# Router logits in four column tiles, exp and the counts out of the ranking's way, and four weight items split in advance

## What is computed

```python
logits = (xt @ w_router + b_router).astype(F32)      # xt (264, 1024), w_router (1024, 8)
top_val, top_idx = lax.top_k(logits, TOP_K)          # TOP_K = 2 of 8 experts
gate = jax.nn.softmax(top_val, axis=-1)
...
counts = jnp.bincount(expert, length=N_EXPERTS)
padded = (counts + MOE_ROWS - 1) // MOE_ROWS * MOE_ROWS      # MOE_ROWS = 128
...
y_rows = lax.map(expert_block, (x_rows, blk_expert))  # swiglu(xb, w_gate[e], w_up[e], w_down[e])
```

## Time and profile before

| | us |
|---|---|
| median of 3 runs | 1290.85 (1290.51 to 1290.99) |
| the profiled execution | 1297.05 |
| its span | 1295.4 |
| busy: PE, DVE, ACT, POOL | 1250.1, 1038.1, 923.4, 78.1 |
| from the end of the attention (466.00) to item 2 of block 0 (521.50) | 55.5 |
| first expert block, from 521.50 | 82.5 |

### The profile page before, as it was taken

One profiled execution on the slowest core, in us unless ns is written; L12 is line 12 of the kernel. 1 busy time (PEld: TensorE's weight loads), 2 busy tenths in 40 slices (PEclk: granted clock), 3 DMA queues, 4 the chain that ended last, 5 costly groups with the idle time before them and its releaser, 6 DMA issues.

```text
span 1295.4 us, 21488 instructions
## 1 busy us (share of the span) xinstructions
PE 1250.1 (96%) x7324; PEld 1068.8 (83%) x7324; DVE 1038.1 (80%) x1463; ACT 923.4 (71%) x1330; POOL 78.1 (6%) x77
## 2 busy tenths in 40 slices
PE   6999999999997989999999999999999999999997
PEld 6989999999975767788888888888888888887885
DVE  6667766567539855998998998997998998998995
ACT  5755454456475774987987987887888888887783
POOL 1000000004301001100000000000000000002600
PEclk9989999999997988999999999999999999999998
DMA  8555445556569545998998998998998998998940
GB/s 350 196 211 193 167 179 196 195 195 241 167 225 381 225 163 200 410 421 338 414 400 325 403 403 319 416 401 323 413 397 328 415 391 330 417 387 323 409 184 34
DMA packets 59999, 391.50 MB, mean 302 GB/s; under 512 B 6718, under 2 KB 12994, under 8 KB 21474
## 3 DMA queue, kind: packets, MB, share of 16 engines
q1 hardware_dynamic: 51298, 354.29, 69.5%
q0 software_dynamic: 8640, 36.40, 7.6%
HBM read 367.41 MB, written 27.45 MB: 305 GB/s over the span
## 4 chain that ended last, share of the span: by engine, by line
PE 81%; DVE 10%; ACT 4%; issue 3%; DMA 1%; DVEq 0%; ACTq 0%; SPq 0%
PE bank L1931 17%; PE bank L1933 17%; PE bank L1932 17%; PE bank L1529 8%; PE bank L1530 8%; PE bank L1531 8%; DVE w_lo L1399 2%; PE bank L1916 1%; DVE d_lo L988 1%; ACT arena L735 1%; DMA ring<-in_wd 1%; ACT w_hi L851 1%; PE bank L1741 1%; PE bank L1865 1%; DVE arena L1226 1%
## 5 line engine op out<-in xcount | busy, mean ns | idle before, releaser
L1399 DVE TENSOR_TENSOR w_lo<-raw,w_hi 128x1024 fp32r<-128x1024 f32 x528 | 623.4, 1223 | 32.9 <-ACT w_hi L851 14.8
L851 ACT CAST w_hi<-raw 128x1024 fp32r<-128x1024 f32 x528 | 543.3, 1056 | 86.8 <-PE bank L1933 85.7
L1931 PE MATMUL bank<-w_hi,xg_hi 128*128 128x512 f32 x704 | 274.9, 391 | 1.6 <-DVE w_lo L1399 1.6
L1933 PE MATMUL bank<-w_hi,xg_lo 128*128 128x512 f32 x704 | 274.4, 390 | 0.0
L1932 PE MATMUL bank<-w_lo,xg_hi 128*128 128x512 f32 x704 | 273.9, 389 | 0.0
L988 DVE TENSOR_TENSOR d_lo<-ring,d_hi 128x1024 fp32r<-128x1024 f32 x120 | 148.1, 1240 | 84.8 <-ACT d_hi L606 81.0
L1529 PE MATMUL bank<-hA_hi,d_hi 128*128 128x264 f32 x640 | 184.6, 288 | 12.4 <-DVE hA_lo L978 8.9
L1530 PE MATMUL bank<-hA_lo,d_hi 128*128 128x264 f32 x640 | 182.1, 285 | 0.0
L1531 PE MATMUL bank<-hA_hi,d_lo 128*128 128x264 f32 x640 | 182.0, 284 | 0.0
L606 ACT CAST d_hi<-ring 128x1024 fp32r<-128x1024 f32 x120 | 125.0, 1045 | 76.2 <-PE bank L1531 68.4
L1931 PEld LDWEIGHTS bank<-w_hi,xg_hi 128*128 128x128 f32 x704 | 132.1, 188 | 29.4 <-DVE w_lo L1399 2.2
(11 more groups left out here) (334 smaller groups left out, 1509.3 us busy)
## 6 DMA issues: line engine op xcount, KB each, us to landing
raw<-in_moe SPq DMA_DIRECT2D x264, 1024.0 KB, 6.6
ring<-in_wd SPq DMA_DIRECT2D x29, 2048.0 KB, 8.4
out_rows<-zeros POOLq DMA_DIRECT2D x1, 6656.0 KB, 39.6
slot_rows<-zeros POOLq DMA_DIRECT2D x1, 6144.0 KB, 26.8
out_rows<-yrow POOLq DMA_DIRECT2D x8, 512.0 KB, 7.1
xs<-slot_rows POOLq DMA_DIRECT2D x7, 512.0 KB, 3.7
arena<-in_cmp_pages POOLq DMA_DIRECT2D x16, 128.0 KB, 3.4
X2v<-in_cmp_pages POOLq DMA_DIRECT2D x16, 128.0 KB, 2.8
```

Of the source, the lines that this page charges most:

```text
L851: nc.scalar.copy(w_hi[:, i % NSPLIT, :], raw[:, u % NRAW, ITEM * (i % 2):ITEM * (i % 2) + ITEM])\
L1399: V.tensor_tensor(w_lo[:, i % NSPLIT, :], raw[:, (i // 2) % NRAW, ITEM * (i % 2):ITEM * (i % 2) + ITEM], w_hi[:, i % NSPLIT, :].bitcast(F3 ...
L1931: T.matmul(out, lhs_hi, hi, start=first, stop=False)
L1933: return T.matmul(out, lhs_lo, hi, start=False, stop=last)
```

## The change

The router's weights are put into a buffer 32 columns wide, of which 8 are used and the rest is zero. Chunk k goes to column tile k % 4, so that the logits lie as four partial sums on partitions 0 to 7, 32 to 39, 64 to 71 and 96 to 103; steps 0 to 3 are issued together behind product 5, steps 4 to 7 behind product 7. Matmuls with a constant that has a one where partition mod 32 is the expert turn them to token rows and sum the four. The ranks are signalled apart from the counts, which go to another bank. The exp is issued behind the first items, and the gates that need it are computed in the last block. `AHEAD` is 4; the count of blocks is read after block 0's rows are rounded.

```diff
-AHEAD = 2
+AHEAD = 4
...
+    put("four", p % 32 == np.arange(NE)[None, :])
...
-        lgT = sb("lgT", [NE, NT])
+        lgT = sb("lgT", [P, NT])
...
             nc.gpsimd.memset(zeros[:], 0.0).then_inc(zeros_ready, 1)
+            nc.gpsimd.memset(wide_router[:], 0.0)
...
             pool.dma_start(kv_out, kvT).then_inc(kv_stored, 16)
+            pool.wait_ge(params_in, 32)
+            nc.gpsimd.tensor_copy(wide_router[:, :, 0:NE], w_router).then_inc(ws_ready, 1)
...
             act.wait_ge(lT_done, 1)
-            nc.scalar.copy(lgT[:, :], MISC[0:NE, 0:NT]).then_inc(lT_ready, 1)
+            nc.scalar.copy(lgT[:, :], MISC[:, 0:NT]).then_inc(lT_ready, 1)
...
-            act.wait_ge(rank_in, 1)
-            nc.scalar.activation(sc[:, :, 4:5], sc[:, :, 3:4], ACT.Exp).then_inc(exp_ready, 1)
...
             for i in range(AHEAD):
                 round_item(0, i)
-            act.wait_ge(blk_ready, 1)
-            last = act.value_load(blkinfo[0:1, MAXB + 1:MAXB + 2], min_val=1, max_val=MAXB - 1)
+            act.wait_ge(rank_in, 1)
+            nc.scalar.activation(sc[:, :, 4:5], sc[:, :, 3:4], ACT.Exp).then_inc(exp_ready, 1)
...
                 n = AHEAD
-                for _ in range(2):
-                    round_item(t, n)
-                    n += 1
                 rows_out(t)
...
             gathered(0, 0, (STAT, T0))
             gathered(0, 1, (STAT, T0))
+            act.wait_ge(blk_ready, 1)
+            last = act.value_load(blkinfo[0:1, MAXB + 1:MAXB + 2], min_val=1, max_val=MAXB - 1)
...
-            dve.wait_ge(exp_ready, 1)
-            settle(V.tensor_scalar(sc[:, :, 5:6], sc[:, :, 4:5], 1.0, None, ALU.add))
-            settle(V.reciprocal(sc[:, :, 6:7], sc[:, :, 5:6]))
-            V.tensor_tensor(sc[:, :, 7:8], sc[:, :, 4:5], sc[:, :, 6:7], ALU.mult)
...
-            counts = MISC[:, 48:56]
+            dve.wait_ge(rank_done, 2)
+            counts = B[0][:, 48:56]
...
             def early_and_last():
+                dve.wait_ge(exp_ready, 1)
+                settle(V.tensor_scalar(sc[:, :, 5:6], sc[:, :, 4:5], 1.0, None, ALU.add))
+                settle(V.reciprocal(sc[:, :, 6:7], sc[:, :, 5:6]))
+                settle(V.tensor_tensor(sc[:, :, 7:8], sc[:, :, 4:5], sc[:, :, 6:7], ALU.mult))
...
-            for i in range(AHEAD):
+            rest_item(0, 0)
+            gathered(0, 0, (STAT, T0))
+            rest_item(0, 1)
+            gathered(0, 1, (STAT, T0))
+            for i in range(2, AHEAD):
                 rest_item(0, i)
             dve.wait_ge(blk_ready, 1)
             last = dve.value_load(blkinfo[0:1, MAXB + 1:MAXB + 2], min_val=1, max_val=MAXB - 1)
-            gathered(0, 0, (STAT, T0))
-            gathered(0, 1, (STAT, T0))
...
-                for _ in range(2):
-                    rest_item(t, n)
-                    n += 1
...
-                i = T.matmul(MISC[0:NE, 0:NT], w_router[:, k, :], hB[:, k, :], start=(k == 0), stop=(k == KC - 1))
+                rows_ = slice(32 * (k % 4), 32 * (k % 4) + 32)
+                i = T.matmul(MISC[rows_, 0:NT], wide_router[:, k, :], hB[:, k, :], start=(k < 4), stop=(k >= 4))
...
-                if c >= 2:
-                    logits(c - 2)
-            logits(KC - 2)
-            logits(KC - 1)
+                if c == 5:
+                    pe.wait_ge(ws_ready, 3)
+                    for k in range(4):
+                        logits(k)
+            for k in range(4, KC):
+                logits(k)
...
-                i = T.transpose(MISC[0:z_ - a_, 8 * u:8 * u + 8], lgT[:, a_:z_], ident[0:NE, 0:NE])
+                i = T.matmul(MISC[0:z_ - a_, 8 * u:8 * u + 8], lgT[:, a_:z_], const("four"), start=True, stop=True)
...
-                T.matmul(out, before[0:r, 0:r], both[t], start=(t == 0), stop=True)
+                i = T.matmul(out, before[0:r, 0:r], both[t], start=(t == 0), stop=True)
+            i.then_inc(rank_done, 1)
+            pe.wait_ge(ht_ready, 1)
             for t, (a, z) in enumerate(spans):
-                i = T.matmul(MISC[:, 48:56], ones[0:z - a, 0:P], both[t], start=(t == 0), stop=(t == 2))
+                i = T.matmul(B[0][:, 48:56], ones[0:z - a, 0:P], both[t], start=(t == 0), stop=(t == 2))
             i.then_inc(rank_done, 1)
```

More of the change, by code:

```diff
@@ L83 @@
                       ("cmpmask", 30), ("sdist", PAST + NS), ("scdist", NS * NCMP), ("negslope", 1),
-                      ("iota", P), ("down8", NE), ("blk", MAXB * NE)])
+                      ("iota", P), ("down8", NE), ("blk", MAXB * NE), ("four", NE)])
 VECTORS, NVEC = layout([("mean", P), ("eps", 2), ("mix0", 8), ("mix1", 8), ("ffn0", 8), ("lng", 8), ("lnb", 8), ("kvn", 8), ("w00", 8)])
@@ L156, in build @@
         tok_rstd = sb("tok_rstd", [P, 4])
+        wide_router = sb("wide_router", [P, KC, 32])
         warm = sb("warm", [1, 2])
```

## The result

| | before | after |
|---|---|---|
| median, us | 1290.85 (5 runs) | 1284.35 (5 runs, 1283.43 to 1287.83) |
| profiled execution / its span, us | 1297.05 / 1295.4 | 1283.69 / 1282.1 |

What follows compares the result with a forecast made beforehand. PE was taken to set the pace in the output projection and blocks, with gains only where it stands still, mainly routing. Terms -2.9 - 3.3 + 0.6 = -5.6 us took 1290.85 to 1285.2 us, range 1283.0 to 1288.0.

Steps and rivals of the forecast that it cites:

- Part 1: Output projection: logits steps grouped by four in column tiles, eight records in 0.6 us; gain 2.9 us.
- Rival 2: Output projection: column tiles of full 128-row contraction overlap badly, gain there only 1.3 us, total 1287.3 us; chance 0.08.
- Part 2: Routing: removing the waits for counts and exp together lets the gather begin earlier; gain 1.15 us.
- Rival 4: Routing: PE's counts or DVE's block info remain the gate and item 4 waits; 1288.5 us, chance 0.06.
- Part 3: Routing into block 0: four items prepared in advance remove PE's wait before item 2; 3.3 us together with Part 2.
- case B: Gather: clock rises earlier, DVE's xg_lo half 0 sets PE's start, item 4 at 520.1; Part 2 and Part 3 gain 4.3.
- the cases: Gather: low clock covers as much as before (gain 2.0 to 3.0 us), or case B (4.3); 3.3 taken.
- rival 3: Gather: clock falls earlier against the work, staying low throughout; Part 2 and Part 3 give 0.1, total 1288.4 us; chance 0.07.
- Part 4: Last block: the gates' three steps in DVE's queue lengthen PE's wait for item 12; cost 0.6 us.
- rival 5: Seven block ends: two casts and rests delay item 4 or yrow, decisive from 0.8 us a block; 1294.4 us, chance 0.05.
- my own sign of being wrong: Expert blocks: the forecast counts as wrong if the period of the blocks moves; it expected the periods as before.
- rival 1: Whole kernel: outcome as forecast, 1285.2 us, its own range 1286.5 to 1284.2; chance 0.74.

Runs made afterwards that it cites:

- kernel 1: On the kernel before, only the router logits in column tiles; 1289.16 us (11 runs), ratio 0.9968.
- kernel 2: On the kernel before, only the exp moved behind the first items and the gates into the last block; 1292.06 us (one run).
- 3: On the kernel before, only the ranks signalled apart from the counts, which go to another bank; 1293.29 us (one run).
- kernel 4: On the kernel before, both routing edits together: exp and gates moved, ranks signalled apart from counts; 1292.33 us, ratio 0.999.
- 9: On the changed kernel, items 62, 63 and 64 of every block issued ahead of the last silu and hm; 1282.96 us (6 runs), ratio 0.9923.
- 11: 9 with the last block's early_and_last and last_weights one step later, gates staying in the last block; 1283.33 us (6 runs), ratio 0.9929.
- Kernel 8: kernel 7 with the last block's remaining small work one loop step later; 1286.64 us (8 runs), ratio 0.9951.
- kernel 10: Kernel 8 and 9 together: gates ahead of the loop, small work later, three items early at block ends; 1282.84 us (6 runs), ratio 0.9920.
- kernel 5: On the kernel before, only the four items in advance with their order in routing and blocks; 1288.17 us (one run).
- kernel 6: The changed kernel with two items in advance as before instead of four; 1288.01 us (12 runs), ratio 0.9959.
- kernel 7: The changed kernel with the gates on DVE ahead of the loop over the blocks instead of in the last block; 1287.82 us (one run).
- kernel 12: kernel 10 with DVE reading the count of blocks ahead of the last two splits instead of behind the gates; 1282.40 us (6 runs), ratio 0.9922.

## Why the prediction was right, and where a size was off

**Part 1, right in every term.** 2.9 us forecast, 2.92 measured, in after and alone in kernel 1. The group was taken at 0.6 us and has 0.59; the price behind it was taken at 0.20 and is 0.20. Steps 4 to 7 and the summing matmuls cost nothing: add 7 to the ranks is 6.81 us in both. Rival 2 (tiles overlap badly) falls. The Trainium skill (TensorEngine Tiling (Array Packing), Restrictions and Gotchas) lists the fast weight load as excluded by column tiling; by the reading of that line that I weighed against row L1674, the group would have taken 0.9 us, and it took 0.59. The summing matmuls are 0.4 us longer on PE than the transposes (0.74 against 0.31), not 0.3, and hidden as forecast.

**Part 2, right.** 1.15 us forecast, 1.24 measured. That both waits must go together was the step to test, and kernels 2, 3 and 4 show it (3.64, 3.48, 2.31). Rival 4 falls with it: block info is done 6.34 us behind the ranks' start, forecast 512.5 - 505.89 = 6.6.

**Part 3, right in its mechanism, mis-sized.** "I take 3.3 for both parts" is the term that was off: parts 2 and 3 gave 1.24 + 1.66 + 1.77 = 4.67 us. It is case B: the clock did not fall in the gather at all, and DVE's xg_lo half 0 releases item 0 (a wait of 0.37 us, named so in the row). The forecast of case B was 4.3; item 4 came 13.86 us behind the ranks where it had 520.1 - 505.89 = 14.2. Most of the difference is the counts: I had DVE begin them 0.25 us late behind PE, but with PE at full clock they were there. The choice between the cases was put at a value between them, where none of the profiles with parts 2 and 3 and the gates left in the last block lies (after, 9 and 11 gained 4.7 us). Kernel 8 against 10 prices the pair: 2.6 us; I had 4.3 - 2.0 = 2.3. The 0.10 us a record at the high clock was read too low: 26 records took the 2.85 us of rows 9, 0.11 each, and after has the same; case B does not hang on it.

**The reason for the clock was the wrong one.** I took a value "towards B since the idle time next to the gather goes", and let the 1.54 us ahead of the ranks stand in rival 3 as the thing "which stays". The kernels show the reverse. In every profile with a low stretch the clock falls amid the ranks or counts, before PE's wait for Gw has begun. Kernel 1 has part 1 and not part 2; its table has the fall at the counts, 2.7 us ahead of the gather:

```profile
500.45:501.20 0.75, 0.74 (x6) 0.74 (x6) 0.00 (x0) 0.73 (x2) 0.00 (x0) 1.00 0.00 0
501.20:504.17 2.97, 1.88 (x13) 1.69 (x13) 1.53 (x10) 2.96 (x4) 0.00 (x0) 0.54 0.00 0
```

So the wait that part 2 removes comes too late to be its cause. And the idle time ahead of the ranks did not stay: in after it is 1.08 us. The six summing matmuls of part 1 take PE longer than the three transposes did, and the ranks wait for DVE all the same. In after:

```profile
492.02 0.74 PE L1845 MATMUL bank<-consts_sb,lgT 128*128 128x8 f32 x6
```

and in kernel 2, with the old transposes:

```profile
497.13 0.31 PE L1840 MATMUL bank<-consts_sb,lgT 8*128 8x8 f32 x3
...
501.31 0.39 PE L1855 MATMUL bank<-lg,consts_sb 128*128 128x8 f32 x2 [1.53 <-DVE sc L1325]
```

Sorted by that idle time: all five profiles with 1.53 or 1.54 us (before, 2 to 5) had the clock low in the routing; of the nine with 1.08 or 1.09 (after, 1, 6 to 12) only kernels 1 and 10 had. The work that I had priced at 0.3 us and found hidden thus goes with 2.6 us of gain. It goes with it and doesn't guarantee it, kernel 10 being the code of kernel 8 up to there. That it is the cause is not shown: it was not tested by changing that idle time alone, and the profiles can be sorted another way too. Kernel 1 has the shorter idle time without part 2, kernel 4 has part 2 without the shorter idle time, and both are low; of the eight profiles with both, seven are high. So having both fits better than the idle time by itself (all six profiles that lack one are low), although PE does the same up to the fall in kernel 1 as in after. Rival 3 (low clock for the whole gather) came true nowhere: in kernel 10 the gather took 8.14 us, with the low clock over its first 5.3 us.

The clock also explains why the parts alone don't add up: kernel 4 gave 0.64 us from the ranks to item 4 and kernel 5 1.57, 2.2 together against 4.67. The missing 2.5 are about its price; kernel 6, with parts 1 and 2 and a high clock, gained 3.5.

**Part 4, right.** +0.6 forecast, 1.55 - 0.96 = +0.59 measured, and 1.58 and 1.59 in kernels 4 and 2, which have the gates there and not the rest. That it is the gates and no other work is shown by kernels 7 and 1, 3, 5 (0.93 to 0.97). The block ends cost nothing by the four items (kernel 5: 94.35), so rival 5 falls.

**Not foreseen.** The block's period is 94.42 us instead of 94.35, 0.5 us over seven blocks. Every kernel with the new logits and the old block ends has it (94.40 to 94.43), kernel 1 among them; none without them has it (94.33 to 94.35). What it does there is open: the part changes no instruction of the blocks, but it adds a buffer and enlarges another, which moves the buffers placed behind them. That was not tried. It stands at no one place: measured from the transposes of xs, the steps of a block in after are 0.01 us later than in before at 27 us, 0.03 at 44 and 0.06 at 86 (means of six blocks), and kernels 9 to 12 keep it in what is left of their block. By its letter my own sign of being wrong ("if the period of the blocks moves") is met, but with less than a tenth of the 0.8 us a block at which rival 5 begins.

**Sum.** Forecast 5.6, measured 6.5 us by the distances: 1.4 more from parts 2 and 3, less 0.4 for the block's period; what else moved cancels to 0.1. Read with this, the median of 1284.35 lies close to the end of rival 1's own range (1284.2). The forecast took the 6.2 us between the profile and the median of before as spread evenly; the profile of before reached add 0 latest of all fourteen (475.07 us), so they can lie ahead of every stretch that was priced, and the sum does not suffer from it.

## What to carry to other kernels

Where two waits end together, try their removal together: the parts alone measured 0 and 0, both measured 1.2 us. Look at what the next engine reads into registers before you put settled work ahead of a loop: a read behind running work was free here and behind a settled step cost 1.5 us, and the trace named another as the cause. Where an engine stands still ahead of small work, look at its clock in more than one profile before you call a low stretch the kernel's own: the same instructions had it in one and not in another. And a wait repeated at each block's end is small in any table (0.8 us of 94), but it was the largest thing left, and its mend needs the last block looked at by itself.

## What the runs showed of the hardware

- Column tiles with the full 128-row contraction: four steps, eight fp32 records of 264 columns with 32-column weights, took 0.59 us on the chain, one step of two records 0.54.
- A register read from a freshly settled queue stood in DVE's timeline as 1.52 us of idle time (kernel 7), of which 0.23 were left when it was moved ahead of two running splits (kernel 12); on ACT there are 0.41 us of idle time at the read in after.
- The granted clock fell to 0.50 in the routing in all five profiles in which PE stood still 1.53 or 1.54 us before the ranks, and in two of nine in which it stood still 1.08; it was low in kernel 10 and high in kernel 8, which have the same instructions up to there, and cost 2.6 us. What decides it is open.
